# First four units of a two-block kernel: from two units at a time to one feature tile at a time

## The reference

```python
n = _rms_norm(h, attn_norm_w[l])               # h * rsqrt(mean(h*h) + EPS) * w
proj = jnp.einsum('bsd,dc->bsc', n, w_in[l])   # w_in is 1024 x 4104
(gq, gk, gv, gg, ga, gb, rq, rk, rv, rg) = jnp.split(proj, split_idx, axis=-1)
```

## Time and profile before

| | |
|---|---|
| median of 3 runs | 1095.38 us (1094.36 to 1095.63) |
| the profiled execution | 1094.5 us, span 1092.6 us |
| PE busy | 1080.2 us, 99% of the span |
| POOL, ACT, DVE busy | 498.8, 458.7, 667.1 us |
| chain that ended last | PE 90%, DVE 5%, ACT 2% |
| first real product of PE | at 7.33 us |
| first product of unit 4 | at 31.48 us |

### The profile page before, as it was taken

How to read it: one execution, slowest core, us unless ns; L and a number is a source line. 1 busy time by engine, 2 the same in 40 slices (tenths; PEclk the granted TensorE clock), 3 DMA queues, 4 the chain that set the end, 5 groups by cost and what they waited for, 6 DMA issues and landing times.

```text
span 1092.6 us, 16148 instructions
## 1 busy us (share of the span) xinstructions
PE 1080.2 (99%) x5882; PEld 874.0 (80%) x5882; DVE 667.1 (61%) x967; ACT 458.7 (42%) x805; POOL 498.8 (46%) x375
## 2 busy tenths in 40 slices
PE   9999999999999999999999999999999999999997
PEld 7788877788888888888888888877778778888786
DVE  6877967328856666666631222458663667986863
ACT  6335421446653333333323334245454543244663
POOL 5443631132645444444444444533247686532541
PEclk9999999999999999999999999999999999999999
DMA  9953531331323232323233235222124222212222
GB/s 248 137 87 68 87 56 24 115 78 39 116 77 116 77 115 77 115 77 115 77 106 106 71 103 165 78 77 79 39 76 117 75 61 78 78 40 78 77 78 78
DMA packets 101722, 97.29 MB, mean 89 GB/s; under 512 B 4896, under 2 KB 95776, under 8 KB 101280
## 3 DMA queue, kind: packets, MB, share of 16 engines
q1 hardware_dynamic: 101232, 95.71, 32.3%
q10 hardware_dynamic: 432, 0.79, 0.2%
HBM read 94.38 MB, written 2.10 MB: 88 GB/s over the span
## 4 chain that ended last, share of the span: by engine, by line
PE 90%; DVE 5%; ACT 2%; issue 1%; POOL 1%; DMA 1%; POOLq 0%; DVEq 0%; SPq 0%; ACTq 0%
PE ps L1947 26%; PE ps L1949 25%; PE ps L1948 25%; PE ps L2502 4%; DVE x_a L1253 1%; PE ps L2167 1%; POOL w_lo L540 1%; DVE acc L1264 1%; DVE conv L1791 1%; PE ps L2437 1%; PE ps L2448 1%; DVE tt L1365 1%; PE ps L2425 1%; PE ps L2217 1%; ACT x_a L678 1%
## 5 line engine op out<-in xcount | busy, mean ns | idle before, releaser
L540 POOL TENSOR_TENSOR w_lo<-raw,w_hi 128x512 fp32r<-128x512 f32 (+1 forms) x330 | 445.0, 1359 | 564.5 <-ACT w_hi L661 564.2
L661 ACT ACTIVATE w_hi<-raw 128x512 fp32r<-128x512 f32 (+1 forms) x330 | 201.1, 620 | 254.5 <-PE ps L1949 236.7
L1947 PE MATMUL ps<-x_a,w_hi 128*128 128x512 f32 x624 | 251.4, 403 | 3.6 <-POOL w_lo L540 2.1
L1948 PE MATMUL ps<-x_a,w_hi 128*128 128x512 f32 x624 | 243.3, 390 | 0.0
L1949 PE MATMUL ps<-x_a,w_lo 128*128 128x512 f32 x624 | 243.3, 390 | 0.0
L1947 PE MATMUL ps<-x_b,w_hi 128*128 128x512 f32 x416 | 162.5, 391 | 0.0
L1949 PE MATMUL ps<-x_b,w_lo 128*128 128x512 f32 x416 | 161.9, 389 | 0.0
L1948 PE MATMUL ps<-x_b,w_hi 128*128 128x512 f32 x416 | 161.9, 389 | 0.0
L1947 PEld LDWEIGHTS ps<-x_a,w_hi 128*128 128x128 f32 x624 | 117.2, 188 | 37.3 <-issue 9.9
L1949 PEld LDWEIGHTS ps<-x_a,w_lo 128*128 128x128 f32 x624 | 117.1, 188 | 25.0
L1948 PEld LDWEIGHTS ps<-x_a,w_hi 128*128 128x128 f32 x624 | 117.3, 188 | 24.6 <-issue 2.2
(11 more groups left out here) (349 smaller groups left out, 1503.2 us busy)
## 6 DMA issues: line engine op xcount, KB each, us to landing
raw<-in_w_up SPq DMA_DIRECT2D x44, 512.0 KB, 4.4
raw<-in_w_in SPq DMA_DIRECT2D x31, 512.0 KB, 8.0
raw<-in_c_w_in SPq DMA_DIRECT2D x24, 512.0 KB, 4.7
raw<-in_a_w_in SPq DMA_DIRECT2D x18, 512.0 KB, 4.5
raw<-in_w_down SPq DMA_DIRECT2D x16, 512.0 KB, 4.3
raw<-in_w_out SPq DMA_DIRECT2D x8, 512.0 KB, 4.5
raw<-in_c_w_out SPq DMA_DIRECT2D x8, 512.0 KB, 4.1
raw<-in_w_down SPq DMA_DIRECT2D x8, 384.0 KB, 3.4
```

Source lines behind the costliest of these rows:

```text
L540: nc.gpsimd.tensor_tensor(ring_half(WL, n), raw_half(n), f32(ring_half(WH, n)), SUB) \
L661: nc.scalar.activation(ring_half(WH, n), raw_half(n), ACT.Copy).then_inc(w_hi, 1)
L1947: mm(out, w_hi_, x_hi_, start=first, stop=False)
L1948: mm(out, w_hi_, x_lo_, start=False, stop=False)
```

## The change

Four edits, all in the first four units and what feeds them.

- **Transfers.** SP alternates one x tile with one weight transfer of one feature tile by 512 columns (all four units). Only x tile 0 stays on ACT's queue.
- **Splits.** One high part (ACT) and one low part (POOL) per feature tile, as 4 x 128 columns for four units. The counts `w_hi` and `w_lo` jump from 0 to 8 with the last feature tile.
- **PE.** For feature tiles 0 to 5: four high x high products, four high x low, four low x high, each group behind its own wait. Tiles 6 and 7 unit by unit, the statistic after unit 0 (ahead of the last 18 products). 11 products of ones instead of 16.
- **Squares.** Written to PSUM banks 4 to 6 (three buffers) instead of two buffers in SBUF. `split_hi(8)` moves ahead of `rstd(0)` on ACT.

The diff, cut to its core:

```diff
@@ loads_before (how often a raw slot was filled)
-        n += 1 if q < 2 else 3 if U6 <= 2 * q < U7 else 2
+        n += 0 if q < 2 else 3 if U6 <= 2 * q < U7 else 2
@@ SP
+            def first_weights(k):
+                sp.dma_start(RAW[:, :, k, :], w_in[k * P:(k + 1) * P, 512:1024]
+                             .rearrange("p (s c) -> p s c", s=2)).then_inc(first_in[k], 16)
...
+            first_weights(0)
+            for k in range(1, KT):
+                sp.dma_start(XT[:, k, :], a["x"][:, k, :]).then_inc(x_in[k], 16)
+                first_weights(k)
@@ POOL
+            for k in range(KT):
+                if k < KT - 1:
+                    gp.wait_ge(first_hi, k + 1)
+                else:
+                    gp.wait_ge(w_hi, 8)
+                ins = nc.gpsimd.tensor_tensor(first_ring(WL, k), first_raw(k), f32(first_ring(WH, k)), SUB)
+                if k < KT - 1:
+                    ins.then_inc(first_lo, 1)
+                else:
+                    ins.then_inc(w_lo, 8)
-            for u in range(1, 14):
+            for u in range(4, 14):
                 unit(u)
@@ ACT
+            def first_tile(k):
+                act.wait_ge(x_in[k], 16)
+                operand_hi(XT[:, k, :], XA[:, k, 0, :], vec("attn_norm_w", k))
+                act.wait_ge(first_in[k], 16)
+                if k >= 4:
+                    act.wait_ge(first_done if k < 7 else half_done, k - 3)
+                ins = nc.scalar.activation(first_ring(WH, k), first_raw(k), ACT.Copy)
...
+            def x_square(k):
+                square(0, k, XT[:, k, :], PS[:, 4 + k % 3, :], buffers=3)
...
+            first_tile(0)
+            for k in range(1, KT):
+                first_tile(k)
+                x_square(k - 1)
+            x_square(KT - 1)
+            split_hi(8)
             table(LN_EXP_SET)
             rstd(0)
-            split_hi(8)
             split_hi(9)
@@ DVE
+            for k in range(KT):
+                operand_lo(k, XT[:, k, :], XA[:, k, 1, :], XA[:, k, 0, :], vec("attn_norm_w", k))
+                if k > 0:
+                    accumulate(0, k - 1, PS[:, 4 + (k - 1) % 3, :])
+            accumulate(0, KT - 1, PS[:, 4 + (KT - 1) % 3, :])
@@ PE
+            def first_units():
+                for k in range(6):
+                    kk = k % 4
+                    pe.wait_ge(first_hi, k + 1)
+                    pe.wait_ge(op_hi, k + 1)
+                    for j in range(4):
+                        mm(PS[:, j, :], WH[:, j, kk, :], XA[:, k, 0, :], start=k == 0, stop=False)
+                    pe.wait_ge(op_lo, k + 1)
+                    for j in range(4):
+                        mm(PS[:, j, :], WH[:, j, kk, :], XA[:, k, 1, :], start=False, stop=False)
+                    pe.wait_ge(first_lo, k + 1)
...
+                for j in range(4):
+                    if j == 1:
+                        stat(0)
+                    for k in (6, 7):
...
-            for _ in range(16):
+            for _ in range(11):
                 mm(PS[:, 7, 0:P], ONES[:, :], ONES[:, :], start=True, stop=True)
```

More of the change, by code:

```diff
@@ L702, in _ @@
             act.wait_ge(ones_ready, 4)
[L704 to L737, removed]
+            def first_tile(k):
[5 more added lines that the diff above has]
+                ins = nc.scalar.activation(first_ring(WH, k), first_raw(k), ACT.Copy)
+                if k < KT - 1:
+                    ins.then_inc(first_hi, 1)
+                else:
+                    ins.then_inc(w_hi, 8)
+            def x_square(k):
[6 more added lines that the diff above has]
+            split_hi(8)
             table(LN_EXP_SET)
             rstd(0)
-            split_hi(8)
             split_hi(9)
@@ L1995, in four_halves, with two_units @@
                     ins.then_inc(half_done, 1)
-            def two_units(q, m, X, k0, j0, fill=None, midway=None):
+            def first_units():
[10 more added lines that the diff above has]
+                    for j in range(4):
+                        ins = mm(PS[:, j, :], WL[:, j, kk, :], XA[:, k, 0, :], start=False, stop=False)
+                        if k == 3:
+                            ins.then_inc(half_done, 1)
+                        elif k < 3 and j == 3:
+                            ins.then_inc(first_done, 1)
+                for j in range(4):
+                    if j == 1:
+                        stat(0)
+                    for k in (6, 7):
+                        if j == 0:
+                            pe.wait_ge(first_hi if k == 6 else w_hi, 7 if k == 6 else 8)
+                            pe.wait_ge(first_lo if k == 6 else w_lo, 7 if k == 6 else 8)
+                            operand(k)
+                        ins = three(PS[:, j, :], WH[:, j, k % 4, :], WL[:, j, k % 4, :],
+                                    XA[:, k, 0, :], XA[:, k, 1, :], False, k == KT - 1)
+                    ins.then_inc(half_done, 1)
+            def two_units(q, m, X, k0, j0, fill=None):
                 for k in range(4):
-                    if k == 0 and midway is not None:
-                        stat(midway)
                     if fill is not None:
@@ L2017, in two_units, with unit @@
                             ins.then_inc(half_done, 1)
-            def unit(u, m, X, fill=None, later=None, mlater=None, midway=None, between=None, third=None):
+            def unit(u, m, X, fill=None, later=None, mlater=None, between=None, third=None):
                 for q in QUADS:
@@ L2022, in unit @@
                         if u == U1:
[L2023 to L2026, removed]
+                            first_units()
                         if q == U1:
@@ L2303, in _ @@
                 else:
-                    unit(u, u, XA, fill=0 if u == 0 else None, midway=0)
+                    unit(u, u, XA)
                 if u == 5:
```

53 lines of the change are left out of this document (11 added, 42 removed).

## The result

The changed kernel took 1100.29 us in the median of 5 runs (1099.14 to 1100.36), the kernel before 1095.12 us (1094.36 to 1095.63) on the same chip: a ratio of 1.0046, with a 95% interval of [1.0034, 1.0058]. It is slower by about 5.2 us. The forecast was 1096.5, its range ended at 1099.0, and "slower by over 0.2%" had a chance of 0.27. The profiled execution took 1100.36 us; its span is 1098.0 us for 1092.6 before, so 5.4 us have to be found inside it. Another 0.4 us lie around the span (2.3 us in the median of the five runs, for 1.9).

The account below looks back on a forecast made before the run. PE, busy for 99% of the span, was taken as the bound: 2.4 us gained at the front and 3.5 lost at unit 4's bank gave +1.1 on 1095.38, so 1096.5 us, range 1094.0 to 1099.0.

Parts of the forecast that it names:

- one long stop ended by DVE: Sign ahead of unit 4: one idle stretch of PE of 2.5 to 4.5 us, ended by DVE.
- Rivals 2, 3 and 4: Pair 2's transfer hidden, 1093.0 us (0.11); DVE bound by PSUM additions, 1101 (0.04); no earlier start of PE, 1097.5 (0.11).
- They were in place 8.2 us after the first issue: Pair 2's transfers on SP: both halves landed 8.2 us after first issue, at 28.5.
- pair 3 follows pair 2 on SP: SP's queue: pair 3 in place at the slowest by 41, before unit 6 asks for it after 43.6.
- a landing of up to 13.8 us: Bound on pair 2's landing: from 7.7 to, by the slowest pair, 13.8 us after the second issue.
- +0.2 to +2.0: Forecast case: PE stops at the bank ahead of unit 4 without a slow restart; chance 0.52.
- by the row alone there is no such charge: Unit 4 after the stop: by the trace row alone, no charge for a slow clock on restart.
- rival 1: Unit 4: PE restarts slowly after the stop, 2.4 us at most, result +1.1 to +3.5, middle 1098.7; chance 0.22.
- +1.1 forecast: Stage end, unit 4's first product: 32.6 for 31.48, with 2.4 us gained at the front and 3.5 lost at the bank.

Follow-up runs that it names:

- experiment 1: Changed kernel with the norm's root (and its table) ahead of the first split of unit 4 on ACT; 1096.87 us, ratio 1.0013 to the kernel before.
- experiment 2: Changed kernel with SP issuing pair 3 only when pair 2 has landed; 1097.21 us, ratio 1.0019 to the kernel before.
- experiment 3: Changed kernel with 24 products of ones into an unused PSUM bank behind the four units; 1097.68 us, ratio 1.0026 to the kernel before.
- Experiment 4: Changed kernel with pair 3 issued only after pair 2 landed and 13 products of ones behind the four units; 1095.90 us, ratio 1.0012 to the kernel before.
- experiment 8: Changed kernel with root first, pair 2's first half early with its own wait, and 16 products of ones instead of 11; 1093.15 us.
- experiment 10: Kernel before with only the squares for the first statistic moved to three PSUM banks; 1094.60 us, ratio 0.9999 to the kernel before.
- experiment 6: Changed kernel with root first and pair 2's first half issued once four feature tiles are split; 1092.53 us, ratio 0.9978 to the kernel before.
- 7: Changed kernel with root first, pair 2's first half issued early, and its split waiting for that half alone; 1092.22 us, ratio 0.9978 to the kernel before.
- experiment 11: Changed kernel with units 4 to 7 reading the columns of units 0 to 3 again; 1096.81 us, ratio 1.0022 to the kernel before.
- experiment 5: Changed kernel with the root ahead of pair 2's split and pair 3 issued only after pair 2 landed; 1093.66 us, ratio 0.9992 to the kernel before.

## Why the prediction was wrong

**What held.** The first product (5.59 for 5.9 to 6.2), no hole ahead of the statistic, squares and additions at 0.58 and 0.69 (for 0.57 and 0.70), POOL at 1.37 (for 1.56), the issue of pair 2 at 19.84 for 20.25, one long stop ended by DVE, and the mechanism of it: experiment 1 moves the root and the releaser changes from DVE to POOL. The four units ended at 28.36 for 29.1, but nothing came of the earlier end, since the stop took it up. From ACT's split to unit 4 the forecast had 4.1 us (28.5 to 32.6), the trace has 34.36 - 30.18 = 4.2. Rivals 2, 3 and 4 didn't happen.

**The first step that failed: "They were in place 8.2 us after the first issue".** That figure was read from pairs behind which no other pair was issued for 6 us or more (before, pair 2 went out at 17.53 and pair 3 at 23.7). The prediction named pair 3 ("pair 3 follows pair 2 on SP") but asked only whether pair 3 came in time, not what it took from pair 2. It gave a landing of up to 13.8 us as a bound and then carried none of it into the +0.2 to +2.0 of the forecast. With the count of split halves jumping to 8 at once, both pairs' conditions are met in the same step, and pair 3 is issued right behind. Both halves were in place 10.3 us after the first issue; with pair 3 held back, 8.4 (experiment 2: this is what shows the cause). The term is short by 2.1 us, of which an issue 0.4 earlier gave some back: 1.1 - 0.4 + 2.1 + 0.1 = 2.9 us, as read.

**The second: "by the row alone there is no such charge".** The clock did fall, which was rival 1 (0.22). Its price of 2.4 us at most was nearly right (2.5 read in the trace, 2.6 in experiment 3), but in part by luck: it was worked out from the start of the program, where the loads are slow while the granted clock reads 1.0, and nothing shows that this slowness has the same cause. The Trainium skill (TensorE: Matmul & The Clock Gate, "Why this matters for your kernels") says that idle gaps between bursts of matmuls send the clock back to its lower level. The trace agrees, with 0.50 in the windows. What failed is the weighing: a trace without a long stop says nothing against a fall, and the slow start of the earlier trace rows was the only row on the matter. The two errors also met: the longer landing made the stop 6.0 us instead of 3.5, and all five runs of the changed kernel have a mean clock of 0.995 to 0.998. With a stop of 3.5 us, as forecast, 9 of 11 runs still lost clock (experiment 2), so the step would have failed with the right landing as well. Either error alone leaves the time inside the stated range of 1094.0 to 1099.0 (1097.2 in experiment 2, 1097.7 in experiment 3); it took both to leave it.

Together: +1.1 forecast, +1.8 from issue, landing and root, +2.5 from the clock, 5.4 in the span. Experiment 4 takes both out and gives +1.3.

**The 0.4 us around the span** were not in the forecast, which carried the 1.9 us of before over. Every kernel with the new first stage has 2.2 to 2.5 us there in the median of its runs (one run of experiment 8 has 4.1), experiment 10 (the old stage with squares in PSUM) 1.9. What they are the profile doesn't show, and no run was made for it.

**The version to keep** is that of experiment 6 or 7: 0.22% below the kernel before, 0.7% below the changed one.

## What to carry to other kernels

When one step of a counter fulfils several conditions, the transfers behind them are issued together: take the landing time from a case with the same company in the queue, not from one with nothing right behind. Whatever waits for a transfer at the head of an in-order engine delays all that stands behind it, so put short work whose inputs come earlier (here a root) in front of the wait. And price a stop of TensorE twice, once as time and once as the clock it may lose.

## What the runs showed of the hardware

How long PE stood still ahead of unit 4 in the profiles, and what the mean granted clock of the runs was:

| kernel | stop in the profile, us | runs with a mean clock of 0.999 or 1.0 |
|---|---|---|
| changed kernel | 5.84 | 0 of 5 |
| experiment 1 | 3.80 | 4 of 11 |
| experiment 2 | 3.49 | 2 of 11 |
| experiment 11 | 2.78 | 1 of 10 |
| experiment 5 | 1.41 | 10 of 11 |
| experiment 6 | 0.85 | 11 of 11 |
| kernel before | 0.8 at most | 79 of the 89 runs near 1095 us |

The stop is that of the one profiled run; in the other runs it may be longer or shorter. A mean clock of 0.998 alone does not show a fall, because the mean also holds the end of the program, after PE's last work: in the profile of experiment 4 the granted clock is 1.0 up to 1090 us and 0.58 and 0.50 in the two windows from there to 1093.6, which makes 0.998. In the rows from the changed kernel to experiment 5 the runs of the two groups are also apart in time, by 0.6 us or more where both occur.

The same kernel keeps its clock in one run and loses it in the next (1094.70 and 1098.97 us in experiment 1), and the clock can fall after PE has gone on (33.7 us in experiment 2, 1.2 us after the restart). What a fall costs differs too: 2.5 us in the changed kernel, where the clock came back at 39.5, and about 1.4 us between the two groups of runs of experiment 2, whose profile has it back at 37.1. An average over few runs of such a kernel is a mixture.

How fast a pair arrives also hangs on what it reads: with columns 512 and 768, just read before, in place of 0 and 256 as many bytes were all in place near 31 us (experiment 11), where the changed kernel still moved 62 to 84 GB/s at 33 to 37. The DMA engines were as busy in both (from 27 to 30 us a share of 0.78 to 1.02 at 244 to 352 GB/s, and of 0.84 to 1.08 at 130 to 207), so the same engine time moved fewer bytes. Whether the columns or the second reading made the difference was not tried.
